# A mixer's shift, keys, decays and first-direction preparation set beside its input projection, whose first eight weight slabs are multiplied in three passes

## The reference

```
h = rmsnorm(x, ln1_w);  p = h @ w_in                    # 14 slabs of 256 columns
p = p + mu * (0.5 * (prev_token(p) + next_token(p)) - p)   # the shift, RWKV columns only
r, k, v, wl_f, wl_b, al_f, al_b, gl = split(p)
w = exp(-exp(-softplus(-(w0 + tanh(wl) @ w2)) - 0.5))   # decays, two directions
a = sigmoid(a0 + al @ a2);  g = sigmoid(gl) @ g2
kk = heads(k * k_k);  kk = kk / max(norm(kk), 1e-12)
k_dir = k * (1 + (a - 1) * k_a);  b = kk * a
y = bidirectional_scan(r, w, k_dir, v, kk, b)           # here in chunks of 128 tokens
...  # GLA on the other columns, w_out, mixture of experts, two layers
ml = split(silu(c) @ w_ada + b_ada)                     # 72 slabs: the "ada" slabs
```

## Time and profile before

| | |
|---|---|
| median of three executions | 3462.8 us |
| profiled execution | 3461.28 us |
| its span, first to last instruction | 3459.1 us |
| PE, DVE, ACT, POOL busy | 93%, 40%, 27%, 10% of the span |
| granted PE clock, mean | 0.964 |
| start to the first projection matmul | 30.0 us |
| projection | 98.6 us |
| projection's end to the first chunk product | 41.6 us |
| GLA and join, to the output projection | 67.4 us |

### The profile page before, as it was taken

One profiled execution on the slowest core, in us unless ns is written; L12 is line 12 of the kernel. 1 busy time (PEld: TensorE's weight loads), 2 busy tenths in 40 slices (PEclk: granted clock), 3 DMA queues, 4 the chain that ended last, 5 costly groups with the idle time before them and its releaser, 6 DMA issues.

```text
span 3459.1 us, 42305 instructions
## 1 busy us (share of the span) xinstructions
PE 3222.1 (93%) x17553; PEld 2357.8 (68%) x17553; DVE 1381.9 (40%) x1894; ACT 921.4 (27%) x1326; POOL 354.5 (10%) x245
## 2 busy tenths in 40 slices
PE   7898968999999799998989998999989998989999
PEld 6677845444443388886756664888868886759899
DVE  0544343000000344456464222444554446753366
ACT  1212121111111322224253112222232224353343
POOL 0031201111110000012201210000000001314100
PEclk9899987999999999999998999999999998999999
DMA  6545353999999522221200221222222222203452
GB/s 236 208 182 232 135 219 153 421 421 421 421 421 421 237 98 94 89 96 61 85 1 37 85 76 72 96 97 97 98 73 94 89 97 74 85 37 147 146 184 96
DMA packets 78307, 556.37 MB, mean 161 GB/s; under 512 B 8529, under 2 KB 10577, under 8 KB 11201
## 3 DMA queue, kind: packets, MB, share of 16 engines
q1 hardware_dynamic: 77296, 549.49, 41.0%
q0 software_dynamic: 848, 4.52, 0.3%
HBM read 552.93 MB, written 1.05 MB: 160 GB/s over the span
## 4 chain that ended last, share of the span: by engine, by line
PE 80%; DMA 8%; DVE 8%; ACT 3%; issue 1%; POOL 0%; DVEq 0%; SPq 0%; POOLq 0%; ACTq 0%
PE bank L576 58%; PE bank L878 10%; DMA ring<-slabs 7%; PE bank L1134 2%; PE bank L709 1%; PE bank L720 1%; ACT ht L1355 1%; PE bank L625 1%; PE bank L717 1%; DVE tiny L2103 1%; PE bank L1222 1%; PE bank L1203 1%; DVE wk L2080 1%; DVE rs L1678 1%; PE bank L592 1%
## 5 line engine op out<-in xcount | busy, mean ns | idle before, releaser
L576 PE MATMUL bank<-hhi,whi 128*128 128x512 f32 (+1 forms) x1408 | 520.5, 370 | 35.9 <-DVE hlo L1685 35.8
L576 PE MATMUL bank<-hlo,whi 128*128 128x512 f32 (+1 forms) x1408 | 515.2, 366 | 0.0
L576 PE MATMUL bank<-hhi,wlo 128*128 128x512 f32 (+1 forms) x1408 | 509.7, 362 | 0.0
L878 PE MATMUL bank<-ring,wk 128*64 128x512 f32 x1872 | 431.0, 602 | 14.8 <-DMA ring<-slabs 14.1
L1665 DVE TENSOR_TENSOR wlo<-ring,whi 128x2048 fp32r<-128x2048 f32 x132 | 298.7, 2288 | 276.0 <-ACT whi L1322 245.6
L576 PE MATMUL bank<-fhl,whi 128*128 128x512 f32 (+1 forms) x1408 | 400.1, 371 | 0.0
L576 PEld LDWEIGHTS bank<-hhi,whi 128*128 128x128 f32 x1408 | 265.3, 188 | 93.5 <-issue 33.5
L1322 ACT ACTIVATE whi<-ring 128x2048 fp32r<-128x2048 f32 x132 | 251.2, 1908 | 263.7 <-PE bank L576 257.0
L878 PEld LDWEIGHTS bank<-ring,wk 128*64 128x64 f32 x1872 | 125.1, 137 | 261.0 <-issue 188.0
L576 PEld LDWEIGHTS bank<-hhi,wlo 128*128 128x128 f32 x1408 | 266.4, 189 | 45.4
L576 PEld LDWEIGHTS bank<-hlo,whi 128*128 128x128 f32 x1408 | 266.7, 189 | 39.4
(11 more groups left out here) (380 smaller groups left out, 4300.6 us busy)
## 6 DMA issues: line engine op xcount, KB each, us to landing
ring<-slabs SPq DMA_DIRECT2D x522, 1024.0 KB, 9.2
wk<-mixp POOLq DMA_DIRECT2D x1, 1040.0 KB, 12.6
xt<-xT SPq DMA_DIRECT2D x1, 1024.0 KB, 6.9
xt<-ctxT POOLq DMA_DIRECT2D x1, 1024.0 KB, 12.5
out<-xt SPq DMA_DIRECT2D x4, 256.0 KB, 2.4
cst<-maskc POOLq DMA_DIRECT2D x1, 960.0 KB, 14.6
cst<-attc POOLq DMA_DIRECT2D x1, 896.0 KB, 16.2
keep<-keepc POOLq DMA_DIRECT2D x1, 320.0 KB, 8.2
```

Source lines behind the costliest of these rows:

```text
L576: last = pe.matmul(o, a, b, start=k == 0, stop=k == len(pairs) - 1)
L878: mm = pe.matmul(o, a, b, start=start, stop=stop)
```

## The change

1. **Three passes for slabs 0 to 7** (`N_SPL = 8`). ACT rounds each slab to one of three buffers `ww` (they lie over KR, VT with Y, and KDS with the tail, which are unused until later). POOL subtracts (eight new instructions ahead of its first chunk instruction). ACT rounds HT to `WHX`, DVE subtracts to `WHL`, both tile by tile. PE makes 48 fp32r matmuls a slab in place of 16 float32 ones. Slabs 8 to 13 stay as they were. ACT's rounding of slab n+3 stands behind its copy of slab n.
2. **The shift slab by slab.** DVE shifts two column tiles behind each of the first seven copies and one behind the eighth; the scaled and squared keys follow the fourth slab.
3. **PE's small products inside the projection.** The key sums stand after slab 6 and the first direction's low-rank products after slab 9, in banks 4 to 7. ACT's tanh, sigmoid and root stand ahead of its copy of slab 8, its decays ahead of copy 10, its exponentials ahead of copy 11. One exponential is written straight into KR (`E2_` is gone).
4. **The ada slabs.** `ADA_KK` (4) and the first direction's `ADA_PREP` (12) are gone, `ADA_GLA` is 16 instead of 8, and so 8 are left for the place before the output projection.
5. Counts of shared semaphores (`w0`, `h0`, `x0`) move up with the new users.

```diff
+N_SPL = 8
-ADA_KK, ADA_PREP, ADA_MAT, ADA_GLA, ADA_GMAT = 4, 12, 1, 8, 8
+ADA_PREP, ADA_MAT, ADA_GLA, ADA_GMAT = 12, 1, 16, 8
...
+        WHX = HLO[:, :, TX:T2]
...
+        whl = over("whl", wk_at, W_BT, KT * TX)
+        WHL = v3(whl, 0, KT, TX)
+        ww = [over(f"ww{i}", wk_at, o, SLAB) for i, o in enumerate((W_KR, W_VT, W_KDS))]
...
+            for n in range(N_SPL):
+                slab_wait(pool, S_WIN + n)
+                pool.wait_ge(sem("whi"), n + 1)
+                pool.tensor_tensor(wlo_of(S_WIN + n), slab(S_WIN + n), ww[n % 3][:, :].bitcast(F32), ALU.subtract
+                                   ).then_inc(sem("wlo"), 1)
             pool.wait_ge(sem("consts"), 64)
...
             for n in range(N_WIN):
-                slab_wait(pe, S_WIN + n)
+                if n < N_SPL:
+                    pe.wait_ge(sem("wlo"), n + 1)
+                else:
+                    slab_wait(pe, S_WIN + n)
                 wait_at(pe, sem("projc"), n - 3)
...
+                    for k in range(KT):
+                        if n == half == 0:
+                            pe.wait_ge(sem("hh"), k + 1)
+                        mm = pe.matmul(o, hi[:, k, c], WHX[:, k, :], start=k == 0, stop=False)
...
+                        pe.matmul(o, lo[:, k, c], WHX[:, k, :], start=False, stop=False)
+                    for k in range(KT):
+                        if n == half == 0:
+                            pe.wait_ge(sem("hl"), k + 1)
+                        mm = pe.matmul(o, hi[:, k, c], WHL[:, k, :], start=False, stop=k == KT - 1)
...
+                if n == 6:
+                    pe.wait_ge(sem("kk"), 1)
+                    for j in range(4):
+                        mm = pe.matmul(b3(4 + j // 2, 2)[:, j % 2, :], BO64, SQM[:, j, :], start=True, stop=True)
+                    mm.then_inc(sem("kks"), 1)
+                if n == 9:
+                    pe.wait_ge(sem("lin"), 1)
+                    pe.wait_ge(sem("kk2"), 1)
+                    lora(0, 4)
...
+            def split_in(n):
+
+                slab_wait(act, S_WIN + n)
+                if n >= 3:
+                    act.wait_ge(sem("slab_used"), S_WIN + n - 2)
+                act.activation(ww[n % 3][:, :], slab(S_WIN + n), ACT.Copy).then_inc(sem("whi"), 1)
+
+            split_in(0)
             act.wait_ge(sem("consts"), 64)
             norm(0, TX)
+            for j in range(KT):
+                act.wait_ge(sem("hn"), j + 1)
+                act.activation(WHX[:, j, :], HT[:, j, 0:TX], ACT.Copy).then_inc(sem("hh"), 1)
+            split_in(1)
+            split_in(2)
...
             for n in range(N_WIN):
+                if n == 8:
+                    act.wait_ge(sem("shifted"), 8)
+                    act.activation(p_tile(12), p_tile(12), ACT.Tanh)
...
                 act.activation(o, b3(n % 4, 2), ACT.Copy).then_inc(sem("projc"), 1)
+                if n + 3 < N_SPL:
+                    split_in(n + 3)
...
+            for j in range(KT):
+                dve.wait_ge(sem("hh"), j + 1)
+                tt_(WHL[:, j, :], HT[:, j, 0:TX], WHX[:, j, :].bitcast(F32), ALU.subtract).then_inc(sem("hl"), 1)
+
+            SH = [v3(ac_, 3072 + 512 * i, 2, TX) for i in range(2)]
+            for n in range(8):
+                dve.wait_ge(sem("projc"), n + 1)
+                w = 2 if n < 7 else 1
+                p, sh = PT_[:, 2 * n:2 * n + w, :], SH[n % 2][:, 0:w, :]
+                tt_(sh[:, :, 1:TX - 1], p[:, :, 0:TX - 2], p[:, :, 2:TX], ALU.add)
+                dve.tensor_copy(sh[:, :, 0:1], p[:, :, 1:2])
+                then(dve.tensor_copy(sh[:, :, TX - 1:TX], p[:, :, TX - 2:TX - 1]))
+                then(stt(sh, sh, 0.5, p, ALU.mult, ALU.subtract))
+                mu = pc("mu", 2 * n, w).rearrange("p (a b) -> p a b", b=1)
+                then(tt_(sh, sh, mu.to_broadcast([P, w, TX]), ALU.mult))
+                tt_(p, p, sh, ALU.add).then_inc(sem("shifted"), 1)
```

More of the change, by code:

```diff
@@ L640, in _, with lora @@
             norm(0, TX)
-            pe.wait_ge(sem("hn"), 8)
+            def lora(d, b0):
+                lo = 64 * d
+                for kind, (wname, tile) in enumerate((("w2", 12), ("a2", 13))):
+                    for j in range(4):
+                        mm = pe.matmul(b3(b0 + 2 * kind + j // 2, 2)[:, j % 2, :],
+                                       mp(wname)[lo:lo + 64, j * P:(j + 1) * P],
+                                       p_tile(tile)[lo:lo + 64, :], start=True, stop=True)
+                    mm.then_inc(sem("lora"), 1)
@@ L660, in _ @@
             mm.then_inc(sem("vtr"), 1)
-            pe.wait_ge(sem("kkd"), 1)
-            pe.wait_ge(sem("vtrc"), 1)
             for d in range(2):
-                pe.wait_ge(sem("lin"), 1)
                 if d:
                     pe.wait_ge(sem("ybc"), 2)
[L669 to L675, removed]
-                ada(ADA_PREP)
+                    lora(1, 0)
+                    ada(ADA_PREP)
                 ts = d
@@ L683, in _ @@
                 mm.then_inc(sem("ktr"), 1)
+                if d == 0:
+                    pe.wait_ge(sem("vtrc"), 1)
                 for step in range(2):
@@ L1727, in _ @@
-            then(tt_(SH, SH, mu.to_broadcast([P, 15, TX]), ALU.mult))
-            tt_(PR15, PR15, SH, ALU.add).then_inc(sem("shifted"), 1)
-            dve.wait_ge(sem("shifted"), 1)
-            for j in range(4):
-                ins = ts_(KK[:, j, :], p_tile(4 + j), pc("kk", j), None, ALU.mult)
-            then(ins)
-            ts_(OMKA, pc("ka", 0, 4), -1.0, 1.0, ALU.mult, ALU.add)
-            tt_(SQM, KK, KK, ALU.mult).then_inc(sem("kk"), 1)
-            ada(ADA_KK)
+            for j in range(KT):
+                dve.wait_ge(sem("hh"), j + 1)
+                tt_(WHL[:, j, :], HT[:, j, 0:TX], WHX[:, j, :].bitcast(F32), ALU.subtract).then_inc(sem("hl"), 1)
@@ new lines, in _ @@
+            SH = [v3(ac_, 3072 + 512 * i, 2, TX) for i in range(2)]
[10 more added lines that the diff above has]
+                tt_(p, p, sh, ALU.add).then_inc(sem("shifted"), 1)
+                if n == 3:
+                    dve.wait_ge(sem("shifted"), 4)
+                    for j in range(4):
+                        ins = ts_(KK[:, j, :], p_tile(4 + j), pc("kk", j), None, ALU.mult)
+                    then(ins)
+                    ts_(OMKA, pc("ka", 0, 4), -1.0, 1.0, ALU.mult, ALU.add)
+                    tt_(SQM, KK, KK, ALU.mult).then_inc(sem("kk"), 1)
@@ L1763, in _ @@
                 carry(CR, CI_, SG_).then_inc(sem("cpre"), 1)
-                ada(ADA_PREP // 3)
+                if d:
+                    ada(ADA_PREP // 3)
                 for j in range(4):
```

100 lines of the change are left out of this document (52 added, 48 removed).

## The result

The changed kernel takes 3445.1 us, the median of five runs (3436.8 to 3447.3), against 3462.8 for the kernel before (five runs, 3454.5 to 3468.3); the ratio over all the runs is 0.9944, with a 95% interval of 0.9926 to 0.9963 (the two medians alone give 0.9949). The forecast was 3440 us. The profiled execution took 3447.3 us, span 3445.5, 13.6 us less than the span before. So the change is worth some 20 us (17.7 and 22.1 by the medians of the two series, 13.6 by the first two profiles), a little more than half of the 35 us that it gains at the start.

A forecast was written before the change was run, and what follows sets the result against it. One chain was taken to bound the first 170 us, a second GLA and the join. First chunk product 35.8 us earlier, less 14.1 us in GLA, gives 21.7 us off: 3440 us, range 3426 to 3453.

The forecast's parts named there:

- the first rival: Projection: DVE gets through beside POOL, the port costs PE nothing, first chunk product at 126.5 us; 3432 us, chance 0.20.
- only (a) goes well: Start of the projection: half of the first rival, DVE's input subtractions escape POOL but its shifts do not; 3436 us.
- (a): Slab 0: DVE's eighth low-half input subtraction meets POOL's first request; POOL taken as first, price 3.2 us, otherwise 0.
- Three passes: Projection slabs 0 to 7: 5.66 us a slab instead of 6.91 in float32, saving at most 10.0 us.
- the clock rival: Split slabs: PE's clock granted at half, each slab 5.66 us more; 3485 us, slower, chance 0.05.
- (b): Shift in the projection: POOL holds DVE's two-input instructions, keys ready at 79.0 us, PE stands from 74.3 to 79.0.
- DVE gets nothing through: Projection: POOL holds the small copies too, keys at 85.2 us instead of 79.0; 15.5 us net, 3446 us, chance 0.14.
- The key sums: After slab 6 in the projection: four key sums are eight records of 0.22 us, 1.8 us.
- The preparation inside the projection: Preparation hidden with 5 us to spare, PE through the projection at 131.6 us, first chunk product at 134.5.
- The ada slabs: GLA's first burst: slabs beyond eight come 2.49 us apart, twenty-fourth not before 43.9 us, output 14.1 us later; end costs nothing.
- GLA's burst is hidden: Rival at GLA: the moved ada slabs cost nothing there, the full 35.8 us is kept; 3426 us, chance 0.08.
- Given back where the experts start: Rival after GLA: the experts wait for slabs, so the gain is given back; 3461 us, chance 0.06.

The follow-up runs named there:

- no_split: Changed kernel with N_SPL = 0: all 14 slabs in float32, PE starting the projection behind all eight input tiles; 3444.1 us, 0.9946 of the kernel before.
- psum_shift: Changed kernel with DVE taking one input of each shift instruction from the PSUM bank instead of ACT's copy; 3431.8 us, 0.9918 of the kernel before.
- before_ada_moved: Kernel before with only the sixteen ada slabs moved to where the change puts them; 3475.3 us, 1.0033 of the kernel before.
- ada_level0: Changed kernel with eight ada slabs in each GLA burst, none at the end, four in each chunk pass at level 0; 3430.7 us, 0.9907 of the kernel before.
- low_by_memset: Changed kernel with POOL writing zeros instead of subtracting, so the weights' low half is left out for eight slabs; 3432.4 us, 0.9917 of the kernel before.
- psum_and_level0: Changed kernel with both the shift's one input from PSUM and four ada slabs at level 0 of each pass; 3423.0 us, 0.9882 of the kernel before.

## Why the prediction was right, and where its steps were off

The two terms of the sum were measured at -35.3 and +15.3 us against -35.8 and +14.1, so -20.0 against -21.7; the medians of two series are 17.7 and 22.1 us below before. The mechanisms named were the ones found: DVE held by POOL, PE standing for the keys, and the slabs at DMA's pace in GLA. That the first term came out to half a microsecond is luck, since three steps in it were off by 1.4 to 3.2 us and cancel. The half of the first rival, "only (a) goes well", did come true, and its gain was taken back elsewhere. By its steps:

- **Three passes.** 5.66 us a slab was right (42.97 to 48.62). Slab 0 took 8.5 us, since at the start its products come at 0.215 us each, clock 0.50 between 27 and 33 us. That is the milder form of the clock rival, in one slab out of eight. From 33 us on the clock is 1.00.
- **The tie, (a), was called wrongly.** DVE's eight subtractions took 2.77 us and ended at 32.5, untouched. They began at 29.74, not at 30.05, so by their pace of 0.34 us the eighth had begun a tenth of a us before POOL, at 32.23. Slab 0's copy came at 36.12 where I had 40.3, and slab 1 began at 37.01, when POOL had its low half ready (forecast 37.1). The term of 3.2 us, the price of the eighth, should have been none.
- **The standstill, (b).** By slab 6 PE was 3.1 us ahead of the forecast (71.2, not 74.3). POOL ended at 67.6, not 70.2, and the keys were ready at 77.2, not 79.0. PE stood 6.1 us, not 4.7. Seven instructions with two inputs had got through or were at it when POOL ended, where I had about eight, and one of POOL's turns went to the small copy (of two numbers a partition; the "four elements" of the prediction are wrong). That is an ingredient of the rival "DVE gets nothing through", and it came to one turn of 4.6 us.
- **The key sums.** 1.8 us forecast, 3.78 measured. This term was mis-sized because I took a full clock for products that stand behind a wait. no_split and psum_shift have 1.73 for the same ones. With this, the errors cancel: PE comes 3.1 us early, stands 1.4 us longer and needs 2.0 us more here, and the sums are through at 81.1 against 80.8.
- **The preparation inside the projection.** Right: the last projection matmul ends at 132.1 (131.6), and 2.9 us later the first chunk product starts, as forecast.
- **The ada slabs.** Twenty-four slabs, the last starting 44.3 us after the first where I had 43.9. The rest of the 1.2 us is their own length at the end, 1.73 to 1.93 us at the lower clock instead of about 1. before_ada_moved and ada_level0 show the term from both sides, 15.5 and 15.3 us. "GLA's burst is hidden" is thereby refuted.
- **"Given back where the experts start"** is refuted by the table: 2955.3 and 2955.5 us from the output projection on.
- **What was not in the sum**: the clock between the first chunk product and GLA, forecast as no change. It cost 6.2 us in the first profile and gave 1.3 in the second; 3.1 of it, in the last pass, stand in both.

On what holds DVE, the runs show four cases beside POOL's subtraction, which reads SBUF: two inputs in SBUF are held (4.99 against 0.69 us), one input in SBUF is held for copy and scale (4.61 against 0.16; 4.99 against 1.14), one of two from PSUM isn't (0.69), a copy from PSUM isn't (0.15). Beside a fill, which only writes, two inputs in SBUF aren't held either (0.69), but a scaling is (0.80 against 0.34). The Trainium skill (SBUF — State Buffer, section "Who interferes with whom") has this list too: two SBUF inputs contend with a GpSimd instruction that reads, not with one that only writes, and copies and scalings contend when they use two ports. The trace agrees in each case by these times; which ports an instruction used it does not show. The same section of the Trainium skill says that whoever is first keeps the pair for the whole instruction. Here it is seen at the last one, where POOL's subtraction ends at 67.59 and DVE's instruction, begun at 63.15, at 68.14, 0.55 us later, which is little less than its own length; between two subtractions about one passes.

What stays open: whether (a) could go POOL's way with a start some tenths of a us later, which was not tried, and why the last pass before GLA is 3.1 us longer. From GLA's output to the end, no_split, low_by_memset and psum_shift took 2982 us in their profiles, and the kernel before, both profiles of the changed one, before_ada_moved, ada_level0 and psum_and_level0 2992, though all run the same instructions there but for eight ada slabs beside the join, in a wait. Nearly all of it (9.8 us between the changed kernel and no_split) lies between 1706 and 1840 us, at the feed-forward stage behind the first attention: stretches of 100 us (columns as above), in the changed kernel and in no_split:

```profile
1800.00:1900.00 100.00, 93.75 (x351) 62.69 (x350) 43.92 (x92) 33.95 (x68) 18.34 (x4) 0.87 0.12 43
```

```profile
1800.00:1900.00 100.00, 93.47 (x386) 61.53 (x385) 46.77 (x100) 36.34 (x73) 18.35 (x4) 0.99 0.11 43
```

The granted clock is 0.87 in one and 0.99 in the other (0.85 in the kernel before, 1.00 in psum_shift). What decides it was not found. It means that the difference of two single profiles of this kernel is good to some 10 us only, and that a step must be read from its own stretch.

## What to carry to other kernels

Work given to POOL to relieve PE took DVE's time with it, as long as both read SBUF: here a saving of 10 us of matmuls came to 2 us by the medians, until DVE read one side from PSUM, where the result still lay, and it came to 12 (11.5 by the profiles, in which slab 1 also starts 3 us earlier). When work is moved away from a critical place, price the place it goes to as a stretch of its own. Slabs beyond those that lie ready cost 2.49 us of DMA each here, however little PE has to do with them. In portions of four, at places that wait anyway, sixteen of them cost 1.1 us in the pass that was looked at, some 4 us in all by that, instead of 15.

## What the runs showed of the hardware that was not expected

- A copy of two columns (128x2, float32, SBUF to SBUF) took 4.61 us beside a subtraction on POOL, as long as an instruction of 512 columns.
- POOL itself is slowed little: 5.11 us for the last subtraction, against 4.62 for the same one in psum_shift, while DVE's took seven times as long.
- After a wait of 6.1 us PE's clock was granted at half for 3.8 us of products, and was full again in the slab behind them.
- Executions of one kernel differ by up to 16 us (3429.5 to 3445.2). The two profiles of the changed kernel show it as clock in the products between the chunk passes; between kernels the clock also differs around 1834 us, without any change in the instructions there.
- The times of one kernel can lie in two groups. The six of psum_shift are at 3424.8 to 3428.0 and at 3435.6 to 3439.7 us, with their median of 3431.8 in the gap, so medians of so few runs are good to some microseconds only.
